# Two-stage transformer block on one core: the end of the mLSTM cells, with normalised heads read from PSUM, a skip product on GpSimd, gate weights prepared further ahead and the first expert load moved

## The reference, cut to what matters

```python
hn = hf * lax.rsqrt(mean(hf * hf) + EPS)                  # per token and head
y_ml = sigmoid(z) * (hn * ml_norm + ml_skip * x_c)         # mlstm_readout
out = (sigmoid(g_mla) * y_mla + sigmoid(g_ml) * y_ml) @ w_out
x = x + g1 * out
aff = softmax(rmsnorm_modulated(x) @ w_router)             # 16 experts, each takes its 32 best tokens
y_e = (silu(xs_e @ w_gate_e) * (xs_e @ w_up_e)) @ w_down_e # 3 x 1024 x 1024 weights an expert
out = rmsnorm(x + g2 * scatter_add(y_e * g_e))
```

## Time and profile before

| | us |
|---|---|
| median of 3 runs | 1912.07 |
| lowest and highest | 1909.53, 1916.52 |
| the profiled execution: its time, its span | 1913.64, 1911.8 |
| PE, DVE, ACT, POOL busy in the span | 1729.0, 837.9, 620.7, 143.1 |

### The profile page before, as it was taken

The page is one execution under the profiler, slowest core; times in us unless marked ns, Lnnn a source line. Parts: engine busy times, 40 slices in busy tenths (PEclk is TensorE's granted clock), DMA queues, the critical chain, the costliest instruction groups (busy, mean ns, idle before and its releaser), DMA issues.

```text
span 1911.8 us, 27848 instructions
## 1 busy us (share of the span) xinstructions
PE 1729.0 (90%) x11962; PEld 1391.9 (73%) x11962; DVE 837.9 (44%) x1286; ACT 620.7 (32%) x890; POOL 143.1 (7%) x88
## 2 busy tenths in 40 slices
PE   9999999999999999999999999999989865666566
PEld 7899888888898899888999998669987321111112
DVE  4532665555435432756666675645675000000001
ACT  2433531544342233531544464543532100000001
POOL 0044100100010244000000020000000000000000
PEclk9999999999999999999999999999999988878878
DMA  6332334677733323336544421202159999999997
GB/s 249 113 108 93 128 113 174 265 308 299 310 119 108 113 89 111 112 113 244 221 177 166 159 99 56 80 23 88 67 231 412 428 427 427 427 427 427 427 427 311
DMA packets 35547, 414.77 MB, mean 217 GB/s; under 512 B 3936, under 2 KB 4192, under 8 KB 4832
## 3 DMA queue, kind: packets, MB, share of 16 engines
q1 hardware_dynamic: 34992, 410.63, 54.7%
q10 hardware_dynamic: 432, 2.36, 0.3%
HBM read 411.93 MB, written 1.05 MB: 216 GB/s over the span
## 4 chain that ended last, share of the span: by engine, by line
PE 70%; DMA 16%; DVE 7%; ACT 4%; another core or an unknown queue 2%; issue 1%; SPq 0%; DVEq 0%; POOL 0%; ACTq 0%
PE ps L209 50%; PE ps L761 7%; PE ps L1573 4%; PE ps L1167 3%; DMA ring<-in_w_e_down_dram 3%; DMA high<-in_w_e_down_dram 3%; DMA high<-in_w_e_gate_dram 3%; DMA low<-in_w_e_down_dram 3%; DMA low<-in_w_e_up_dram 3%; DMA ring<-in_w_e_up_dram 2%; ACT high L203 2%; DVE high L168 2%; DVE rring L168 1%; PE ps L1195 1%; PE ps L806 1%
## 5 line engine op out<-in xcount | busy, mean ns | idle before, releaser
L209 PEld LDWEIGHTS ps<-rarena 128*128 128x128 f32 x3648 | 447.6, 192 | 15.9 <-DVE low L168 7.8
L209 PE MATMUL ps<-rarena 128*128 128x256 f32 (+1 forms) x3648 | 457.8, 288 | 0.1
L209 PE MATMUL ps<-rarena,rring 128*128 128x256 f32 (+1 forms) x2352 | 326.8, 295 | 9.4 <-ACT low L203 4.9
L209 PEld LDWEIGHTS ps<-rarena,rring 128*128 128x128 f32 x2352 | 300.0, 194 | 21.9 <-DVE rring L168 7.1
L203 ACT ACTIVATE high<-ps 128x256 f32<-128x256 f32 (+2 forms) x188 | 91.0, 484 | 513.0 <-PE ps L1573 198.5
L203 ACT ACTIVATE rarena<-ring 128x2048 fp32r<-128x2048 f32 x76 | 140.4, 1847 | 238.8 <-PE ps L209 187.6
L168 DVE TENSOR_TENSOR rarena<-ring,rarena 128x2048 fp32r<-128x2048 f32 x76 | 168.9, 2223 | 106.9 <-ACT rarena L203 105.3
L168 DVE TENSOR_TENSOR high<-high,ps 128x512 f32<-128x512 f32 x52 | 35.8, 688 | 316.4 <-PE ps L1573 265.8
L1573 PE MATMUL ps<-high,low 128*32 128x512 f32 x576 | 89.4, 750 | 48.4 <-DMA high<-in_w_e_up_dram 27.0
L168 POOL TENSOR_TENSOR rring<-ring,rring 128x1024 fp32r<-128x1024 f32 x44 | 104.3, 2370 | 272.8 <-ACT rring L203 271.9
L761 PE MATMUL ps<-high 128*128 128x128 f32 (+4 forms) x1014 | 118.9, 294 | 2.0 <-DVE high L190 1.5
(11 more groups left out here) (207 smaller groups left out, 1781.8 us busy)
## 6 DMA issues: line engine op xcount, KB each, us to landing
ring<-in_w_in_dram SPq DMA_DIRECT2D x68, 1024.0 KB, 4.8
ring<-in_w_ffn_up_dram SPq DMA_DIRECT2D x22, 2048.0 KB, 9.1
high<-in_w_e_gate_dram SPq DMA_DIRECT2D x18, 2048.0 KB, 49.3
high<-in_w_e_up_dram SPq DMA_DIRECT2D x18, 2048.0 KB, 49.1
high<-in_w_e_down_dram SPq DMA_DIRECT2D x18, 2048.0 KB, 49.9
ring<-in_w_mod_dram SPq DMA_DIRECT2D x12, 2048.0 KB, 8.0
ring<-in_w_e_up_dram SPq DMA_DIRECT2D x9, 2048.0 KB, 49.6
ring<-in_w_e_down_dram SPq DMA_DIRECT2D x9, 2048.0 KB, 50.2
```

The source lines that it names most:

```text
L209: ins = self.e.matmul(out, l, r, start=first and i == 0, stop=end and i == n - 1)
```

## The change

- `parts_of_weights2`: up to tile 11 two tiles ahead as before, at tile 12 two tiles (14 and 15) in one step, from then on three ahead (`WIDER_LEAD = 12`). `AHEAD` is 6, so steps 40 to 45 stand behind the cells and only tile 23 behind the transposes. After the cells PE's banks for the gates are 6, 7, 4, 5 in place of 6, 7.
- The turned heads go to banks 0 to 3, two tiles in each, and stay there. DVE makes a tile of `T.yT` in two operations: times ml_norm and times `T.sgz`, read from PSUM, which frees the bank after its second tile (`yt0` to `yt3`), and then plus `T.ymla`. ACT's four copies are gone. The factor 0.5 moves into the gm operation of `out`.
- The skip branch: GpSimd multiplies `T.xs` by `T.sgz` (8 operations, `skipped`) and adds the product to `T.ymla` for tiles 0 to 4; for tiles 5 to 7 DVE adds it in `out` (`gs0` to `gs7`).
- `T.AE` of two chains lies in `T.xm`, which leaves slot 6 free in the cells. Expert load n = 0 goes there ahead of the weights of tile 18. `gates2.pe` is awaited at n = 4, `yT7` at n = 7.

```diff
--- before.py
+++ after.py
@@ -513,7 +513,9 @@
         free_to(mark_b)
         T.SC = alloc(2, 4, 256)
         heads = [(d, q) for q in range(2) for d in range(2)]
-        T.AE = {k: alloc(4, 256) for k in heads}
+        T.AE = {k: shaped(xf[:, 2048 + 1024 * i:3072 + 1024 * i], (4, 256)) if i < 2 else alloc(4, 256)
+                for i, k in enumerate(heads)}
+        assert place["top"] <= LOW + 11392
         T.hsq = at(24576, 256)
         T.hn = spare.rearrange("p (t n) -> p t n", t=2)
         assert place["top"] <= LOW + 19584
@@ -699,6 +701,9 @@
             for u, (nm, i, ld, c0, z) in enumerate(UNITS2):
                 if u == 8:
                     load("qkblk", (lambda t: t[:, 0:2048], a["qk_blocks"]))
+                if u == 18:
+                    S.wait_ge("v1.pe")
+                    load("e0gate0", (lambda t: t, a["w_e_gate_2"][0, 0]), at=6)
                 if z == 0:
                     columns(ld, a["w_in_2"], 8, c0, 256)
             columns("to0", a["w_out_2"], 8, 0, 512)
@@ -710,13 +715,16 @@
                 for nm in ("gate", "up", "down"):
                     for k in range(8):
                         if n == 0:
-                            S.wait_ge("v1.pe")
+                            n += 1
+                            continue
                         if n == 1:
                             S.wait_ge("cells.pe", "cells.v", "cells.a")
                         if n == 2:
                             columns("to1", a["w_out_2"], 8, 512, 512)
                         if n == 4:
-                            S.wait_ge("yT7", "gates2.pe")
+                            S.wait_ge("gates2.pe")
+                        if n == 7:
+                            S.wait_ge("yT7")
                         i, src = order[n % len(order)], a[f"w_e_{nm}_2"][g_, k]
                         if n < 95:
                             load(f"e{g_}{nm}{k}", (lambda t: t, src), at=i)
@@ -1443,13 +1451,16 @@
 
             mix([cell(d, q) for d, q in heads], fill, CE_PLAN, False)
             PE.mark("cells.pe")
+            pool["p"] = [6, 7, 4, 5]
             mix([iter(range(AHEAD))], fill, [1], False)
+            yt = [take_bank(j, f"yt{j}.ps", f"yt{j}") for j in range(4)]
             for t in range(2):
                 PE.wait_ge(f"hn{t}")
-                for hh in range(2):
-                    b = take("m", f"yt{t}{hh}.ps", f"yt{t}{hh}")
-                    transposes([(b[:, 128 * i:128 * i + 128], T.hn[:, t, 512 * hh + 128 * i:512 * hh + 128 * i + 128])
-                                for i in range(4)]).then_inc(*PE(f"yt{t}{hh}.ps"))
+                for j in range(4):
+                    ins = transposes([(yt[j][:, 256 * z + 128 * t:256 * z + 128 * t + 128],
+                                       T.hn[:, t, 256 * j + 128 * z:256 * j + 128 * z + 128]) for z in range(2)])
+                    if t:
+                        ins.then_inc(*PE(f"yt{j}.ps"))
             mix([], fill, [1])
             PE.mark("gates2.pe")
             w = halves(wslot("to0")[:, 0:4096], 8)
@@ -2097,11 +2108,6 @@
             A.act(T.ss, T.ss, Ln, scale=1.0 / 256, bias=misc(1)).then_inc(*A())
             A.act(T.ss, T.ss, Exp, scale=-0.5).then_inc(*A("ss"))
             mix([none(AHEAD)], fill, [1], False)
-            for t in range(2):
-                for hh in range(2):
-                    A.wait_ge(f"yt{t}{hh}.ps")
-                    take_copy(T.yT[:, 4 * hh:4 * hh + 4, 128 * t:128 * t + 128], v4(ps(f"yt{t}{hh}.ps"))).then_inc(
-                        *A(f"yt{t}{hh}"))
             mix([], fill, [1])
             A.e.preload_act_table(ACT.Sqrt)
             for i in range(8):
@@ -2723,18 +2729,21 @@
                     if nm == "gm":
                         V.wait_ge(f"gm{i}", f"z{i}")
                         g = T.gtm[:, i % 2, :]
-                        V.ts(g, g, 1.0, add).then_inc(*V())
+                        V.ts(g, g, 1.0, add, 0.5, mul).then_inc(*V())
                         V.stt(T.sgz[:, i, :], T.sgz[:, i, :], 1.0, g, add, mul).then_inc(*V(f"gz{i}"))
                     if nm == "ga":
                         V.wait_ge(f"ga{i}", f"ao{i}")
                         V.stt(T.ymla[:, i, :], T.gtm[:, i % 2, :], 1.0, T.ymla[:, i, :], add, mul).then_inc(*V(f"gy{i}"))
+                        if i >= SKIPS_ON_G:
+                            V.wait_ge("skipped")
+                            V.tt(T.ymla[:, i, :], T.ymla[:, i, :], T.xs[:, i, :], add).then_inc(*V(f"gs{i}"))
 
                 for u in range(len(UNITS2)):
                     yield
                     if u:
                         out(*UNITS2[u - 1][0:2])
-                    if u + 2 < len(UNITS2):
-                        parts_of_weights2(u + 2)
+                    for v in range(u + (2 if u <= WIDER_LEAD else 3), min(len(UNITS2), u + (2 if u < WIDER_LEAD else 3) + 1)):
+                        parts_of_weights2(v)
                     yield
                 out(*UNITS2[-1][0:2])
 
@@ -2874,16 +2883,15 @@
                     V.ts(hv, hv, T.ss[:, t, hd:hd + 1], mul).then_inc(*V())
                 V.mark(f"hn{t}")
             mix([none(AHEAD)], fill, [1], False)
-            V.wait_ge("yt11")
             for i in range(8):
                 y = T.yT[:, i, :]
-                V.wait_ge(f"xs_{i}")
-                V.stt(y, y, pc("ml_norm_2", i), T.xs[:, i, :], mul, add).then_inc(*V())
-                V.tt(y, y, T.sgz[:, i, :], mul).then_inc(*V())
+                V.wait_ge(f"yt{i // 2}.ps")
+                V.stt(y, ps(f"yt{i // 2}.ps")[:, 256 * (i % 2):256 * (i % 2) + 256], pc("ml_norm_2", i), T.sgz[:, i, :],
+                      mul, mul).then_inc(*V(f"yt{i // 2}") if i % 2 else V())
                 if i > 3:
                     mix([none(2)] if i < 7 else [], fill, [1], i == 7)
-                V.wait_ge(f"gy{i}")
-                V.stt(y, y, 0.5, T.ymla[:, i, :], mul, add).then_inc(*V(f"yT{i}"))
+                V.wait_ge(f"gs{i}")
+                V.tt(y, y, T.ymla[:, i, :], add).then_inc(*V(f"yT{i}"))
             V.tt(E.gg, sc2, pc("norm2_2", 0, 8), mul).then_inc(*V("gg"))
             V.tt(wrt, wrt, E.gg.unsqueeze(2).to_broadcast([128, 8, 16]), mul).then_inc(*V("wrt"))
             for lo, hi_ in ((0, 4), (4, 5), (5, 6), (6, 7), (7, 8)):
@@ -2998,6 +3006,13 @@
             folded("1n2", F.sq)
             folded("z1", fin_sq)
             folded("fin", T.m1sq)
+            for i in range(8):
+                G.wait_ge(f"xs_{i}", f"gz{i}")
+                G.tt(T.xs[:, i, :], T.xs[:, i, :], T.sgz[:, i, :], ALU.mult).then_inc(*G())
+            G.mark("skipped")
+            for i in range(SKIPS_ON_G):
+                G.wait_ge(f"gy{i}")
+                G.tt(T.ymla[:, i, :], T.ymla[:, i, :], T.xs[:, i, :], ALU.add).then_inc(*G(f"gs{i}"))
 
         for final in (False, True):
             if not final:
@@ -3049,7 +3064,8 @@
 
 ST_LATE = 6
 AT_PLAN = 2 * [0, 0] + 2 * [0, 1] + 5 * [0, 0, 0, 1] + [1, 0, 1, 1, 1, 0, 1, 1]
-AHEAD = 4
+AHEAD = 6
+WIDER_LEAD, SKIPS_ON_G = 12, 5
 QK_STEPS = 3
 CE_PLAN = [1, 1, 0] * 14
```

## The result

The changed kernel takes 1920.88 us in the median of 10 runs (1919.14 to 1926.74), the kernel before 1912.9 us in 10 runs beside it (1907.93 to 1916.52). The ratio is 1.0056, 95% interval [1.0045, 1.0066]: slower by 10.7 us, [8.6, 12.6]. The profiled execution of the changed kernel was the longest of its ten, 1926.74 us with a span of 1924.9.

What follows compares the result with a forecast made beforehand. The prediction took the final expert-weight stream, started by the engine chain ending at E, to bound the kernel. Terms 2.06 + 2.7 + 2.0 + 1.7 = 8.5 us on 1912.07 gave 1920.6 us, range 1910 to 1926.

Steps and rivals of the forecast that it cites:

- The bound: Final stream of expert weights, 85 loads in 421 us: the end moves with E, microsecond for microsecond, if E is later.
- E: Issue of expert load n = 11, when PE's first product with expert weights ends; predicted as the end of an engine chain.
- ceiling for a gain: Stream's start: no more than 1.7 + 4.95 = 6.6 us can be gained, as the stream would then be full.
- 1.7 us of a dry stream ahead of E: Time for which the expert stream was said to run dry in front of E, read from 1476 to 1480.
- The extra tile: In the cells at step 25, DVE also makes tile 15's parts while PE waits for a bank: +2.06 us.
- Bank 3: Ahead of `to0`: PE takes banks 0 to 3 together and waits for tile 7's first operation: +2.7 us.
- The first rival: Banks do not hold PE, so `to0` starts when tile 23 is done: 1910.3 us, chance 0.13.
- The clock on `to0`: PE's idle 7.6 us ahead of `to0` lowers its clock for up to 5 us: +2.0, bounds 0 and 2.5.
- GpSimd: Six of thirteen GpSimd operations beside DVE's chain, 0.56 us each, half taken: +1.7 us, bounds 0 and 3.4.
- The second rival: GpSimd takes the SBUF from DVE for its whole duration, 6 x 0.72 = 4.3 us: 1923.2 us, chance 0.08.
- PSUM read at no extra cost: DVE's eight `yT` operations reading PSUM: 484 ns against 0.48 us from SBUF, so nothing added to the sum.
- The early load: Expert load n = 0 issued earlier fills the slots some 5 us sooner; worth nothing while E is late.

Runs made afterwards that it cites:

- g_three_late: f_three with the first expert load put back behind the loads of `to0`; ratio 1.0007 against the kernel before.
- k_before: The kernel before, unchanged, profiled a second time: 142.5 us from the first constant-matrix products of the cells (M0) to E, 432.9 us from E to the end.
- i_lead9: Changed kernel with the second weight tile at tile 9 in place of tile 12; ratio 1.0035 against the kernel before.
- c_nopool: Changed kernel without GpSimd's 13 operations, so the skip product is missing from the result; ratio 1.0030 against the kernel before.
- a_banks: Changed kernel with the first half of w_out (`to0`) in banks 4 to 7, which do not hold the turned heads; ratio 0.9998 against the kernel before.
- h_busy17: Changed kernel with 34 constant products (7.5 us) on PE in its wait ahead of `to0`; ratio 1.0037 against the kernel before.
- j_late: Changed kernel with the first expert load put back behind the loads of `to0`; ratio 1.0049 against the kernel before.
- f_three: Changed kernel with `to0` in banks 4 to 7, second tile at tile 9, no GpSimd work, three DVE operations per `yT` tile; 1906.96 us, ratio 0.9977.
- b_lead: Changed kernel with weight tiles two ahead throughout, `AHEAD` left at 6; ratio 1.0057 against the kernel before.
- d_busy: Changed kernel with 24 constant products (5.3 us) on PE in its wait ahead of `to0`; ratio 1.0040 against the kernel before.

## Why the prediction was right or wrong

**The bound.** Right. The stream behind E has the same length to 0.4 us in eleven profiles, and the time follows E, as long as E is late enough for the stream to run dry. g_three_late shows where that ends: E 4.0 us sooner than before, time 1.3 us longer. The prediction's ceiling for a gain, from one more load in the stream, is the same limit, but its 1.7 us of a dry stream ahead of E were misread. The stretch 1476 to 1480 lies mostly behind E. In the 4 us ahead of E the stream ran at 406 GB/s, in the 4 us behind it at 264, and this second figure is much the same in k_before and in the changed kernel (281, 254): it is the start of the new loads, not a reserve.

**The extra tile, +2.06.** Measured 2.0 (i_lead9 and the landmark), in the place and by the wait that was named. Missed: the longer wait is followed by a low clock of PE in some executions, which costs 1.4 to 1.6 us in the two profiles that show it.

**Bank 3, +2.7.** The step was right: `to0` waits for the first operation of tile 7. The stretch from the scalings to `to0` grew by 4.7 us: 2.7 is the order of the work, 1.4 GpSimd beside DVE, and about 0.5 small gaps ahead of DVE operations that wait for another engine, of some 0.1 us each, that I had added up without (c_nopool, 16.8 us where my sum gives 16.3). a_banks prices the whole choice of banks at 11 us between the ratios (9.3 between the E shifts, the clock in the cells taken out). The first rival, had the banks not held PE, was put at 1910.3 us, 10.3 under the forecast; a_banks is 11 under the changed kernel. PE's idle time in this wait was put at 7.6 us and measured 7.71.

**The clock on `to0`, +2.0.** Measured 2.3 (h_busy17), in the first 6 us. The two levels showed as 0.50 and 1.00.

**GpSimd, +1.7.** Mis-sized: 3.3. I counted six operations beside DVE's chain, and these were the right six: four in the cells, where DVE is on the chain from 1398 on (1.9 of the 3.3), and two behind them. What failed is the half. I took it that DVE's operation would come first in half of the cases and lose nothing, but each of the six lengthened DVE's work, by 0.40 us or by 0.56. Where DVE's cast had started first (ahead of 1398.86, 1408.03 and 1429.45), GpSimd's operation ran on into the subtraction behind it, and that took 0.40 us more. The other 0.4 us are DVE's waits for GpSimd's results, which I had put at nothing. The bounds, 0 to 3.4, were wide enough, and the price of one is about the one that the row showed. The second rival's 0.72 us for each was not seen: 0.57 is the most.

**PSUM read at no extra cost.** Right: 484 ns in the eight new operations, 485 ns in the eight of the kernel before that read SBUF in their place, and the trace still does not show the 65 ns that the Trainium skill would add (VectorE: DVE Perf Modes, section on the TRN2 errata).

**The early load, nothing.** Right for this kernel (j_late), as was its reason. It would be worth a full load once E is early (f_three against g_three_late).

**The sum.** 8.5 predicted, 10.7 measured [8.6, 12.6]. With the sizes as measured: 2.0 + 2.7 + 0.5 + 2.3 + 3.3 = 10.8, and 1.6 more in executions with the low clock in the cells. That the forecast's median, 1920.6, is only 0.3 from the measured 1920.88 is luck: the kernel before ran at 1912.9 and not 1912.07 beside it, and medians differ by 8.0 where the ratio gives 10.7. Nor does the agreement of 10.8 with 10.7 prove every term, as the shift of E in the profiles stands above the ratio throughout (see what stays open).

**Expectations that were wrong.** b_lead's: I had treated the lead and `AHEAD = 6` as two edits. d_busy's: `to0` was to take 13.8 us and took 15.7, because 2.58 us of wait were left. g_three_late's: 1.7 us of gain were to remain, which is 0.9991, and the interval begins at 0.9998; the 1.7 us were the misread reserve above. f_three's stretch from M0 to the first expert product, 136 to 137 us, was 138.0, 1.3 of it the low clock. k_before's 435.0 us did not repeat.

**What stays open.** In every run the E shift of the one profile is 1.3 to 3.5 us above the shift by the ratio (leaving g_three_late aside). A common cause would lie in the kernel before, either ahead of M0 or behind E, where its two profiles differ by 2 us. Two profiles don't settle it. Nor do the runs say why the clock behind the waits in the cells falls in some executions alone.

## What to carry to other kernels

When data stay longer in PSUM, look at who takes those banks next and whether it takes them all at once: here VectorE saved 0.46 us a tile, and TensorE started `to0` 7 us later than with other banks. Put two operations of preparation into a pause of the engine that does them; the same second tile cost nothing at tile 9 and 2.0 to 3.6 us at tile 12. And before a transfer is moved forward, look whether the DMA engines are idle at the point that sets the stream's start: where they were, an earlier load bought nothing that could be told (j_late), and where they were not, it bought its whole duration (f_three against g_three_late).

## What was not expected of the hardware

- A wait of TensorE of 2.6 us was followed by the low clock in some executions and not in others: in d_busy, in two of six profiles with the wait of 2.6 us for a bank in the cells, and in five of all thirteen profiles behind a second wait of 2.56 to 2.58 us in the cells, for ScalarE, which the kernel before has too. In d_busy the fall came in the first 2 to 4 us behind the restart (0.86, then 0.50, then 0.79 in 2 us steps); behind the second wait of the changed kernel it was there at once, with the first 12 products in 2.93 us and not 1.68. Where GpSimd works this second fall costs nothing (58.0 us from PE's restart to the scalings with it in a_banks and without it in d_busy); in f_three it costs 1.3 us. Waits of 0.4 to 0.7 us ahead of `to0` left the clock at 1.00.
- A GpSimd operation of 128x256 beside a VectorE operation that reads and writes SBUF can lengthen both: 0.69 to 1.25 and 1.23 to 1.63 us on VectorE, 0.73 to 1.18 on GpSimd. All six that stood on VectorE's chain did.
